# Attention scores from stacked rounded halves, and stick-breaking weights as a running product of sigmoids

## The reference

```
p = rmsnorm(x) @ w_in                    # 1024 tokens, 1024 -> 3072 columns
qa, ka, va, qb, kb, vb = split(p)        # 512 columns each
# group A: 4 heads, two score maps of 64 columns each
s  = q @ k.T / 8 ; p_c = softmax(mask(s)) for c in 0, 1 ; w = p_0 - lam * p_1 ; o = rmsnorm(w @ v) * 0.8
# group B: 8 heads of 64 columns, strictly causal
z        = q @ k.T / 8
log_keep = where(mask, log_sigmoid(-z), 0)
suffix   = cumsum(log_keep, reverse=True)             # along the keys
a        = where(mask, exp(log_sigmoid(z) + suffix - log_keep), 0)
o        = a @ v
x = x + concat(oA, oB) @ w_out
x = x + peer(rmsnorm(x))                 # 128^2 experts, top 16 per head, 8 heads
```

## Time and profile before

| | |
|---|---|
| time, median of 3 (range) | 3598.82 us (3597.29 to 3598.83) |
| profiled execution, its own time | 3593.81 us |
| its span, first to last instruction | 3592.0 us |
| busy PE, DVE, ACT, POOL | 3372.0, 2401.5, 1048.7, 1655.2 us |
| project / attend A / attend B | 0 to 316 / 316 to 541 / 541 to 840 us |

### The profile page before, as it was taken

The page is one execution under the profiler, slowest core; times in us unless marked ns, Lnnn a source line. Parts: engine busy times, 40 slices in busy tenths (PEclk is TensorE's granted clock), DMA queues, the critical chain, the costliest instruction groups (busy, mean ns, idle before and its releaser), DMA issues. The chain is left out here.

```text
span 3592.0 us, 45109 instructions
## 1 busy us (share of the span) xinstructions
PE 3372.0 (94%) x17090; PEld 2942.4 (82%) x17090; DVE 2401.5 (67%) x4484; ACT 1048.7 (29%) x1158; POOL 1655.2 (46%) x847
## 2 busy tenths in 40 slices
PE   7998989998899999999999999995899999999998
PEld 5886656666788999999899989995688888888886
DVE  2401658883311788999999999996567666666665
ACT  3221336652211222333333333332112211221120
POOL 2420000001211356555445544565787777877773
PEclk9997877778999999999999999997999999999999
DMA  3132000003221367666666766788887778777874
GB/s 126 70 115 101 24 24 12 12 1 135 80 88 45 137 206 234 206 239 238 236 234 227 241 232 239 251 321 320 308 295 284 289 289 305 283 286 283 310 277 160
DMA packets 252449, 697.16 MB, mean 194 GB/s; under 512 B 20208, under 2 KB 86640, under 8 KB 245104
## 3 DMA queue, kind: packets, MB, share of 16 engines
q1 hardware_dynamic: 178544, 426.35, 33.6%
q0 software_dynamic: 73728, 268.47, 21.1%
HBM read 564.72 MB, written 130.02 MB: 193 GB/s over the span
## 5 line engine op out<-in xcount | busy, mean ns | idle before, releaser
L1150 PE MATMUL hid_ps<-side_hi,u_hi 128*128 128x384 f32 x2048 | 531.3, 340 | 19.8 <-POOL u_lo L836 10.5
L845 POOL DMA_INDIRECT found<-in_u,pick_u x232 | 330.3, 1424 | 425.0 <-DVE found L1081 389.9
L1878 PE MATMUL part<-v_hi,act_hi 128*128 128x512 f32 x1536 | 475.1, 391 | 50.6 <-POOL act_lo L1801 48.8
L1150 PE MATMUL hid_ps<-side_lo,u_hi 128*128 128x384 f32 x2048 | 522.5, 336 | 0.0
L1150 PE MATMUL hid_ps<-side_hi,u_lo 128*128 128x384 f32 x2048 | 522.5, 336 | 0.0
L1878 PE MATMUL part<-v_lo,act_hi 128*128 128x512 f32 x1536 | 474.2, 390 | 0.0
L1878 PE MATMUL part<-v_hi,act_lo 128*128 128x512 f32 x1536 | 473.7, 390 | 0.0
L836 POOL TENSOR_TENSOR u_lo<-u_raw,u_hi 128x1024 fp32r<-128x1024 f32 x128 | 327.5, 2559 | 264.4 <-ACT u_hi L795 263.8
L1817 DVE TENSOR_TENSOR acc<-acc,part 128x1024 f32<-128x1024 f32 x192 | 234.3, 1220 | 307.0 <-PE part L1878 306.9
L1150 PEld LDWEIGHTS hid_ps<-side_hi,u_hi 128*128 128x128 f32 x2048 | 366.8, 189 | 20.5 <-POOL u_lo L836 10.7
L1796 POOL TENSOR_TENSOR v_lo<-v_raw,v_hi 128x2048 fp32r<-128x2048 f32 x64 | 295.8, 4622 | 186.0 <-ACT v_hi L1769 185.4
(11 more groups left out here) (197 smaller groups left out, 5415.5 us busy)
## 6 DMA issues: line engine op xcount, KB each, us to landing
u_raw<-in_uT SPq DMA_DIRECT2D x128, 512.0 KB
v_raw<-in_v SPq DMA_DIRECT2D x64, 1024.0 KB
hid_d<-hid SPq DMA_DIRECT2D x128, 384.0 KB
gate_d<-stage SPq DMA_DIRECT2D x48, 1024.0 KB, 5.6
act_in<-hid_d SPq DMA_DIRECT2D x64, 768.0 KB, 7.6
gate_in<-gate_d SPq DMA_DIRECT2D x32, 1536.0 KB
w_raw<-in_w_in SPq DMA_DIRECT2D x6, 2048.0 KB, 8.3
w_raw<-in_wq SPq DMA_DIRECT2D x4, 2048.0 KB, 8.5
```

Of the source, the lines that this page charges most:

```text
L845: pool.indirect_dma_start(found[:, g], None, u_d, bass.IndirectOffsetOnAxis(ap=pick_u[:, g, n:n + 1], axis=0))\
L1150: mm = pe.matmul(hid_ps[:, s % 2, half, 0:W], w[:, s % 2, ch], x[:, ch, GB * P + half * W:GB * P + (half + 1) * W], start=n == 0, stop=n = ...
L1878: last = pe.matmul(part[:, n % BANKS, cols], a[:, s, j, rows], v[:, s, j, cols], start=j == 0 and m == 0, stop=j == J - 1 and m == 2)
```

## The change

The projections write q and k as rounded halves. `attend` loads them stacked: 128 rows, the upper 64 q_hi, the lower 64 q_lo, against k_hi in both halves of the rows, and against k_lo in both halves; the two products add up in PSUM. In group B two sigmoids and a running product replace the logarithms; the copies of the pieces move from VectorE to ScalarE; the V product takes the 128 columns of both heads of a pair, and half of its output is used. The lines below are the core; buffer and semaphore names that follow from it are left out.

```diff
 project
-        st = sb("st", [P, 4, HALF])
+        st = sb("st", [P, 2, HALF])
+        st_hi = sb("st_hi", [P, 2, HALF], R)
+        st_lo = sb("st_lo", [P, 2, HALF], R)
...
+        def kind_index(n):
+            return sum((w[0] == "v") == (stores[n][0][0] == "v") for w, _ in stores[:n])
 def store(n):                                            # SP
+                m = kind_index(n)
+                sp.wait_ge(st_ok, n + 1)
+                if what[0] == "v":
...
+                    return
-                sp.dma_start(out, st[:, n % 4]).then_inc(st_out[n % 4], 16)
+                sp.dma_start(hi_d[pair][:, cols], st_hi[:, m % 2].bitcast(F)).then_inc(qk_out[m % 2], 16)
+                sp.wait_ge(st_lo_ok, m + 1)
+                sp.dma_start(lo_d[pair][:, cols], st_lo[:, m % 2].bitcast(F)).then_inc(qk_out[m % 2], 16)
 def out_slot(n):                                         # ScalarE
-                if n >= 4:
-                    act.wait_ge(st_out[n % 4], 16 * (n // 4))
+                if m >= 2:
+                    act.wait_ge((v_out if is_v else qk_out)[m % 2], (16 if is_v else 32) * (m // 2))
 def store_low(n):                                        # VectorE, new
+                dve.wait_ge(st_ok, n + 1)
+                dve.scalar_tensor_tensor(out=st_lo[:, m % 2], in0=src, scalar=HD ** -0.5 if what == "qb" else 1.0,
+                                         in1=st_hi[:, m % 2].bitcast(F), op0=ALU.mult,
+                                         op1=ALU.subtract).then_inc(st_lo_ok, 1)
...
+                if g == 1:
+                    store_lows("qa")                      # before the norm of ka
...
+            for what in ("ka", "qb", "kb"):
+                store_lows(what)
 TensorE
+                    if (n - 4) // ITEMS in (3, 4):
+                        pe.wait_ge(st_lo_ok, n - 4 - ITEMS + 1)
-                        if pair >= 2:
-                            pe.wait_ge(st_ok, STORED_BEFORE[g] + 2 * (pair - 1))
+                        if pair >= 2 or g == 2:
+                            pe.wait_ge(st_lo_ok, ITEMS * (g - 1) + 2 * (pair - 1))
 attend, SP
-                sp.dma_start(qT[:, n % 2], qT_d[n]).then_inc(qk_in[n % 2], 16)
-                sp.dma_start(kT[:, n % 2], kT_d[n]).then_inc(qk_in[n % 2], 16)
+                for part in range(2):
+                    s = 2 * (n % 2) + part
+                    rows = slice(part * HD, part * HD + HD)
+                    for half, q_d in enumerate((q_hi_d, q_lo_d)):
+                        here = slice(half * HD, half * HD + HD)
+                        sp.dma_start(q_both[here, s].bitcast(F), q_d[n][rows]).then_inc(qk_in[n % 2], 16)
+                        sp.dma_start(k_hi[here, s].bitcast(F), k_hi_d[n][rows]).then_inc(qk_in[n % 2], 16)
+                        sp.dma_start(k_lo[here, s].bitcast(F), k_lo_d[n][rows]).then_inc(qk_in[n % 2], 16)
 attend, ScalarE, group B
-                act.activation(soft[:, n % 2, w], z_ps(n)[:, w], ACT.Abs).then_inc(abs_ok, 1)
-                ... Exp(scale=-1), Ln(bias=1), and in weights(n): Exp
+                act.activation(soft[:, n % 2, w], z_ps(n)[:, w], ACT.Sigmoid, scale=-1.0).then_inc(left_ok, 1)
+                if n >= 3:
+                    act.wait_ge(tb_ok, pieces_before(units_b, n - 2))
+                act.activation(take[:, n % 3, w], z_ps(n)[:, w], ACT.Sigmoid).then_inc(take_ok, 1)
+            take_pieces_b(n - 2) moves here from VectorE, as ACT.Copy
 attend, VectorE, group B: weights(n) takes the place of logs(n)
-                dve.scalar_tensor_tensor(... max(z, 0) + soft ...)
-                dve.tensor_tensor_scan(logw[:, n % 2, w][:, ::-1], ones[:, w], soft[:, n % 2, w][:, ::-1],
-                                       0.0, ALU.mult, ALU.subtract).then_inc(scan_ok, 1)
-                dve.tensor_tensor(logw[:, n % 2, w], z_ps(n)[:, w], logw[:, n % 2, w], ALU.add)
+                dve.tensor_tensor_scan(chain[:, 1:w + 1], soft[:, n % 2, 0:w][:, ::-1], ones[:, 0:w],
+                                       1.0, ALU.mult, ALU.mult).then_inc(scan_ok, 1)
+                dve.wait_ge(scan_ok, n + 1)
+                dve.wait_ge(take_ok, n + 1)
+                dve.tensor_tensor(take[:, n % 3, 0:w], take[:, n % 3, 0:w], chain[:, 0:w][:, ::-1],
+                                  ALU.mult).then_inc(a_ok, 1)
 attend, TensorE
-                    pe.matmul(out[:, a:b], q, kT[rows, buf, a:b], start=True, stop=True)
+                    pe.matmul(out[:, a:b], q, k_hi[:, s, a:b], start=True, stop=False)
+                    pe.matmul(out[:, a:b], q, k_lo[:, s, a:b], start=False, stop=True)
+                (the diagonal block likewise: k_hi, k_lo, then the mask as before)
-                    pe.wait_ge(log_ok, n - z_before(i) + 1)
+                    pe.wait_ge(take_ok, n - z_before(i) + 1)
-                        last = pe.matmul(out, v[:, b, 512 + h * HD:512 + (h + 1) * HD], wT[:, at % 4, j],
+                        last = pe.matmul(out, v[:, b, both], wT[:, at % 4, j],     # both: 128 columns
```

More of the change, by code:

```diff
@@ L99, in project @@
         st_ok = sem("st_ok")
-        st_out = [sem(f"st_out{n}") for n in range(4)]
+        st_lo_ok = sem("st_lo_ok")
+        v_out = [sem("v_out0"), sem("v_out1")]
+        qk_out = [sem("qk_out0"), sem("qk_out1")]
         block = c.enter_context(nc.Block())
@@ L152, in _ @@
                 store(n)
-            for n in range(4):
-                sp.wait_ge(st_out[n], 16 * len(stores) // 4)
+            for n in range(2):
+                sp.wait_ge(v_out[n], 16 * ITEMS)
+                sp.wait_ge(qk_out[n], 32 * 2 * ITEMS)
         @block.gpsimd
@@ L265, in _, with store_low, store_lows @@
             heads = "p b (h d) -> p b h d"
+            def store_low(n):
+                what, k = stores[n]
+                m = kind_index(n)
+                if what[1] == "a":
+                    src = tr_ps[:, k // 2 % 2, 4 * (k % 2):4 * (k % 2) + 4].rearrange("p a b -> p (a b)")
+                else:
+                    src = pr_ps[:, k % 4]
+                dve.wait_ge(st_ok, n + 1)
+                dve.scalar_tensor_tensor(out=st_lo[:, m % 2], in0=src, scalar=HD ** -0.5 if what == "qb" else 1.0,
+                                         in1=st_hi[:, m % 2].bitcast(F), op0=ALU.mult,
+                                         op1=ALU.subtract).then_inc(st_lo_ok, 1)
+            def store_lows(what):
+                for k in range(ITEMS):
+                    store_low(stores.index((what, k)))
             for g in range(2):
@@ L1214, in attend @@
         unit = sb("unit", [P, P], R)
-        qT = sb("qT", [P, 2, T])
-        kT = sb("kT", [P, 2, T])
+        q_both = sb("q_both", [P, 4, T], R)
+        k_hi = sb("k_hi", [P, 4, T], R)
+        k_lo = sb("k_lo", [P, 4, T], R)
         v = sb("v", [P, TB, D])
         prob = sb("prob", [P, 3, 2, T])
-        soft = sb("soft", [P, 2, T])
-        logw = sb("logw", [P, 2, T])
+        soft = prob[:, 0]
+        take = prob[:, 1:3].rearrange("p a b t -> p (a b) t")
+        chain_even = sb("chain_even", [P, T + 2])
         ones = sb("ones", [P, T])
@@ L1403, in _ @@
                 if n < NB:
[L1404 to L1406 removed]
+                    breaks(n)
+                if 2 <= n <= NB + 1:
+                    take_pieces_b(n - 2)
                 if n >= 7 and (n - 3) % 4 == 0:
@@ L1505, in _, with weights @@
                 mix_low(HEADS_A - 1, half)
-            def logs(n):
+            def weights(n):
                 h, i = units_b[n]
[L1510 to L1516, removed]
-                dve.tensor_tensor_scan(logw[:, n % 2, w][:, ::-1], ones[:, w], soft[:, n % 2, w][:, ::-1],
-                                       0.0, ALU.mult, ALU.subtract).then_inc(scan_ok, 1)
-                dve.wait_ge(scan_ok, n + 1)
[L1520 to L1533, removed]
+                w = (i + 1) * P
+                dve.wait_ge(left_ok, n + 1)
+                chain = chains[n % 2]
+                if n == 1:
+                    dve.memset(chain[:, 0:1], 1.0).then_inc(chain_set, 1)
+                if n < 2:
+                    dve.wait_ge(chain_set, n + 1)
+                dve.tensor_tensor_scan(chain[:, 1:w + 1], soft[:, n % 2, 0:w][:, ::-1], ones[:, 0:w],
+                                       1.0, ALU.mult, ALU.mult).then_inc(scan_ok, 1)
+                dve.wait_ge(scan_ok, n + 1)
+                dve.wait_ge(take_ok, n + 1)
+                dve.tensor_tensor(take[:, n % 3, 0:w], take[:, n % 3, 0:w], chain[:, 0:w][:, ::-1],
+                                  ALU.mult).then_inc(a_ok, 1)
             def mix_low_b(k):
@@ L1552, in _, with scores @@
         def _(pe):
-            def scores(out, rows, buf, i, kind):
-                q = qT[rows, buf, i * P:(i + 1) * P]
+            LOADED = 16 * 12
+            def scores(out, s, i, kind):
+                q = q_both[:, s, i * P:(i + 1) * P]
                 for a, b in spans(i):
-                    pe.matmul(out[:, a:b], q, kT[rows, buf, a:b], start=True, stop=True)
```

(19 more changed lines are left out.)

69 lines of the change are left out of this document (38 added, 31 removed).

## The result

The changed kernel takes 3451.93 us (median of 4 executions, 3450.06 to 3454.92) against 3598.06 (3595.53 to 3598.83) for the kernel before on the same chip: 0.9596 of its time, interval 0.9579 to 0.9612. The forecast was 3485 with a likeliest range of 3455 to 3515.

What follows compares the result with a forecast made beforehand. Attention was taken as bound by PE, its plain float32 scores and their low clock. Group A -35, group B -96, projections +16, table load +1 made -114 us: 3480, or 3485 as timed; likeliest 3455 to 3515, 8 in 10 3435 to 3545.

Steps and rivals of the forecast that it cites:

- The 2 us a head for the clock: Group B: allowance for spells at the low clock, raising a head from 22.8 to 24.8 us.
- I keep the 0.46: Scores: 0.46 us of mask and hand-overs per 640-key part, taken over unchanged from the old 64-row scores.
- The larger engine of each turn: Group B: per turn the larger of PE's and VectorE's times, summed to 21.4 us a head.
- Attention is bound by PE, by the plain float32 scores and by the clock that it has under them: Both attention stages: what limits the kernel before; PE busy 192 of 218 and 276 of 299 us, clock 0.75 and 0.72.
- PE's wait for V: Start of group A: a new stall of 9 us until V's transfer lands, bounds 0 and 12.
- VectorE comes late next: Group A: VectorE as the next limit, 31 us a head against PE's 28; larger engine per turn gives 36.8.
- The 10 us stall on the low halves near 181: Projections after g=2: ka's stores queue behind the 2 MB weight load, so PE's last pair starts 10 us late.
- The shorter ones: Projections: shorter stalls on low halves; after g=1 PE's last pair waits for the fourth, about 4 us later.
- The clock that stays low: Rival: PE stays at 1.2 GHz through both attention stages, A 256 and B 319 us, about 3667 in all; 5%.
- the flipping one: Rival: the clock keeps flipping as now, PEclk 0.75 to 0.8, A 214 and B 235 us, 3541 in all; 18%.
- ScalarE changes its table: Rival in group B: 128 table loads between sigmoid and copy, 164 us, B 310 us, 3592 in all; 3%.
- All warm: Rival: full clock throughout, A 172 and B 182 us, projections +8, 3438 in all; 12%.

Runs made afterwards that it cites:

- e3: The changed kernel with every score matmul over the first 64 rows only and q's low half left out: 3486.56 us, ratio 0.9689.
- e2: The kernel before, plain 64-row float32 scores kept, with group B's new sigmoid chain, copies on ScalarE and 128-column V products: 3502.41 us, ratio 0.9728.
- e1: The changed kernel with group B's old logarithm chain, old copies and 64-column V products put back: 3547.18 us, ratio 0.9859.
- e6: The changed kernel with the load of the fourth column group's weights issued two items later: 3445.20 us, ratio 0.9577.
- e7: The changed kernel with pair loads as 6 transfers into 128 partitions, k read twice by a leading dimension of two: 3665.71 us, ratio 1.0184.
- e4: The changed kernel with group B's V products back on 64 columns of weights: 3460.10 us, ratio 0.9612.
- e11: The changed kernel with pairs loaded by 6 plain transfers of 128 partitions, q and k not stacked: 3442.94 us, ratio 0.9575.

## Why the prediction was right, and where it was off

**Group B: right mechanism, mis-sized by 35 us (203 forecast, 168 measured).** Three terms were too large. (1) The 2 us a head for the clock were not needed: 1.00 from 538 to 680. That is 16 us. (2) "I keep the 0.46" took the hand-over of 64-row weights for full ones. For 640 keys 0.99 was forecast and 612.27-611.45 = 0.82 measured: 0.17 for each of eight blocks, 1.4 us a head, 11 in all; e3 has the old 0.99. (3) The larger engine of each turn was summed, as if no turn's slack could be used in the next; with the first two gone (21.4 us a head), 0.8 us a head remain; that they come from this no run tests. The durations themselves were right: sigmoid, running product and multiplication each within 15 ns of their rows at the longest shape.

**"Attention is bound by PE, by the plain float32 scores and by the clock that it has under them": wrong for B.** e2 leaves the scores and has B at 203 us; e1 leaves the chain and has 265. The busy 276 of 299 us misled: at a clock of 0.72 a PE that is often kept waiting looks busy, and VectorE's 30 us a head, 239 of the 299, were the chain behind it. The forecast was still right in sign, since both parts were in the change; that it named the lesser part as the bound cost it nothing here, which is luck.

**Group A: 189 forecast, 190.6 measured, by two errors that cancel.** V landed 43.3 us after the first issue, not 32.8: the prediction took the rate of the earlier trace rows, measured with destinations of 128 partitions, and the pairs now go into 64 at 219 GB/s. The mask came 18.2 us after it instead of 12, and PE's wait for V was 13.1 instead of 9. Against that the time after V's landing was 147.3 us and not 156.5, and there the term is the head: 39.5 us forecast, 35.6 and 35.9 measured from one norm to the next (L1512 at 416.22, 451.82 and 487.71). In these VectorE is busy for 29.9 and 30.0 us and PE for 29.1 and 29.8, so that VectorE comes late next fits, but it leads by little.

**Projections: +18.9 for +16.** The 10 us stall on the low halves near 181 is the 9.6 us above, and e6 shows its cause in the queue of the weights' load. The shorter ones sum to 5.8 for about 4. The other 3.5 us go with the clock: 0.97 in the projections where it was 1.00, and PE busy for 4.9 us more with the same 1280 instructions.

**The rivals.** The clock that stays low (5%) and the flipping one (18%) fell, group B by the widest margin; ScalarE changes its table once, not 128 times. "All warm" had B at 182 and A at 172: B was warmer and tighter than that, A was not, because its start has no work for PE. The Trainium skill (TensorE: Matmul & The Clock Gate, Part 4) says that transposes don't engage the full clock. In B a fifth of PE's work is transposes, by the forecast's own count, and the clock stays at 1.00: here the trace does not show the loss that the rival expected from that rule.

**The +4.1 us behind attention** are no effect of the change that can be told from chance. From the first instruction of `route` on, all code is unchanged, and this part lasts 2751.8 us before and 2755.8 after, but anything from 2750.9 (e1) to 2763.4 (e7) in the fourteen traces. So a difference of a few us between two of these kernels is better read from the windows of attention than from the whole time.

## What to carry to other kernels

A busy engine at a low clock is not yet the bound: ask which chain made it pause before the clock fell, and run each part of a double change alone, in which the part that looked secondary brought two thirds here. Stages that start with loads pay for bytes, for the form of the transfers (most likely the partitions that they reach) and for the order in one queue: what is needed first goes first, in parts, and each copy of an operand is a load. Keep successive matmuls at one weight shape, and price a shape by a stretch in which it alternates with its neighbours, not by a run of equals.

## What the hardware showed that was not expected

- A change of weight shape between matmuls costs 0.11 to 0.18 us: 64 against 128 rows 0.32 to 0.14 and 0.99 to 0.82 us (e3, after), 64 against 128 columns 0.80 to 0.69 and 1.89 to 1.71 (e4, after).
- With scores of 64 rows the clock stayed at 0.50 for 26 us with PE full (e3, 380 to 406) and for 24 us at the start of B (e3, 544 to 568); with scores of 128 rows it was back within about 6 us of PE's start in both places. Once it was back, 64-row scores didn't lower it (e2, 1.00 from 566 to 736).
- DMA in transfers of 256 KB into 64 partitions: 219 GB/s with all engines busy; of 512 KB into 128: 379 (e11). With an outermost dimension of 2: 58 GB/s (e7).
